# Rows of two weight loads shared out unevenly over the transfer engines, a load in halves and a combination moved ahead, in a fused decoder step

## The reference

```python
def run(args):
    xb, e = args
    z = xb @ w_up[e] + b_up[e]
    x_glu = jnp.minimum(z[:, ::2], SWIGLU_LIMIT)
    x_lin = jnp.clip(z[:, 1::2], -SWIGLU_LIMIT, SWIGLU_LIMIT)
    y = x_glu * jax.nn.sigmoid(SWIGLU_ALPHA * x_glu) * (x_lin + 1.0)
    return y @ w_down[e] + b_down[e]
...
out = jnp.zeros((T + 1, D_MODEL), jnp.float32).at[buf_tok].add(yb * buf_w[:, None])[:T]
```

## Time and profile before

| | |
|---|---|
| time, median of 3 runs | 1134.8 us (1134.33 to 1135.38) |
| the profiled execution's own time | 1134.97 us |
| its span, first to last instruction | 1133.2 us |
| granted PE clock, mean | 0.999 |
| PE busy | 1103.4 us (97%) |
| DVE, ACT, POOL busy | 28%, 20%, 3% |
| moved by DMA | 437.99 MB, mean 387 GB/s |

### The profile page before, as it was taken

The page is one execution under the profiler, slowest core; times in us unless marked ns, Lnnn a source line. Parts: engine busy times, 40 slices in busy tenths (PEclk is TensorE's granted clock), DMA queues, the critical chain, the costliest instruction groups (busy, mean ns, idle before and its releaser), DMA issues.

```text
span 1133.2 us, 14624 instructions
## 1 busy us (share of the span) xinstructions
PE 1103.4 (97%) x5774; PEld 491.7 (43%) x5774; DVE 313.6 (28%) x794; ACT 228.7 (20%) x635; POOL 34.6 (3%) x71
## 2 busy tenths in 40 slices
PE   9999999999999999999999999999999999999997
PEld 6788878844243333333433333333332323233322
DVE  6565662122212121213221313030303021212123
ACT  3663454412020101010101010111110101010103
POOL 1200012200000000000000000000000000000000
PEclk9999999999999999999999999999999999999999
DMA  9743528999999999999999999999999999999995
GB/s 349 292 162 116 166 105 341 408 397 421 429 427 430 436 427 430 433 429 431 422 426 434 427 431 436 428 430 437 428 430 436 429 430 436 429 426 428 427 423 235
DMA packets 31263, 437.99 MB, mean 387 GB/s; under 512 B 5616, under 2 KB 7944, under 8 KB 10360
## 3 DMA queue, kind: packets, MB, share of 16 engines
q1 hardware_dynamic: 30592, 435.64, 91.7%
q10 hardware_dynamic: 624, 1.68, 0.4%
HBM read 436.00 MB, written 2.41 MB: 387 GB/s over the span
## 4 chain that ended last, share of the span: by engine, by line
PE 73%; DMA 22%; DVE 2%; issue 1%; ACT 1%; SPq 0%; DVEq 0%
PE bank L1407 26%; DMA ring<-in_experts 21%; PE bank L1445 16%; PE bank L1113 10%; PE bank L1159 5%; PE bank L1303 4%; PE bank L1282 3%; PE bank L1227 1%; PE bank L1316 1%; PE bank L1306 1%; DVE area L1861 1%; PE bank L1279 1%; PE bank L984 1%; PE bank L995 1%; DMA ring<-in_opening 1%
## 5 line engine op out<-in xcount | busy, mean ns | idle before, releaser
L1407 PE MATMUL bank<-ring,area 128*64 128x512 f32 x1872 | 424.7, 597 | 7.3 <-DMA ring<-in_experts 6.9
L1407 PEld LDWEIGHTS bank<-ring,area 128*64 128x64 f32 x1872 | 126.6, 136 | 276.2 <-issue 254.0
L1445 PE MATMUL bank<-ring,area 128*64 128x512 f32 x960 | 220.6, 599 | 5.9 <-DMA ring<-in_experts 5.8
L1849 DVE TENSOR_TENSOR x_tok<-x_tok,bank 128x512 f32<-128x512 f32 x60 | 41.3, 688 | 326.6 <-PE bank L1303 326.6
L862 ACT ACTIVATE area<-area 128x256 f32<-128x256 f32 x64 | 26.7, 417 | 513.7 <-DVE area L1861 513.7
L1113 PE MATMUL bank<-ring 128*128 128x264 f32 (+1 forms) x512 | 119.6, 391 | 0.0
L1445 PEld LDWEIGHTS bank<-ring,area 128*64 128x64 f32 x960 | 63.5, 136 | 122.8 <-issue 107.2
L1113 PEld LDWEIGHTS bank<-ring 128*128 128x128 f32 x512 | 95.8, 190 | 20.0 <-issue 1.3
L1886 DVE TENSOR_TENSOR area<-area 128x1024 f32<-128x1024 f32 x15 | 18.4, 1225 | 209.5 <-ACT area L872 209.5
L1303 PE MATMUL bank<-area 128*128 128x512 f32 x128 | 71.8, 644 | 0.0
L1159 PE MATMUL bank<-area,ring 128*128 128x264 f32 x256 | 58.6, 387 | 0.0
(11 more groups left out here) (292 smaller groups left out, 685.6 us busy)
## 6 DMA issues: line engine op xcount, KB each, us to landing
ring<-in_experts SPq DMA_DIRECT2D x64, 4096.0 KB, 24.9
ring<-in_experts SPq DMA_DIRECT2D x36, 2048.0 KB, 30.4
ring<-in_experts SPq DMA_DIRECT2D x24, 1024.0 KB, 9.0
ring<-in_w_in SPq DMA_DIRECT2D x16, 1024.0 KB, 9.5
area<-in_experts SPq DMA_DIRECT2D x7, 2048.0 KB, 13.1
area<-in_experts SPq DMA_DIRECT2D x3, 4096.0 KB, 20.8
ring<-in_w_out SPq DMA_DIRECT2D x8, 1024.0 KB, 4.8
area<-in_experts SPq DMA_DIRECT2D x4, 1024.0 KB, 8.3
```

The source lines that it names most:

```text
L1407: m = mm(bank[2 * h + n][64 * e:64 * e + 64, :], xe[:, k, 64 * e:64 * e + 64], w[:, kk, e, NB * n:NB * (n + 1)], start=False, stop=(k == K ...
L1445: m = mm(bank[4 + c][64 * e:64 * e + 64, :], y_t[:, 4 * half + f, 64 * e:64 * e + 64], w[:, f, e, :], start=False, stop=(half == 1 and f = ...
L1849: eng.tensor_tensor(x, x, combined_bank(unit, last)[:, :], ALU.add).then_inc(s.added, 1)
```

## The change

Three edits, all for the last pair.

- Loads 185 and 186 become three transfers each: rows 0 to 111, rows 112 to 119 and rows 120 to 127, all on the load's own semaphore, which is now counted to 48 (`signals` gives 3).
- Load 188 becomes two transfers, its first and its second half of columns; the second counts on a semaphore of the opening (`open_loaded[0]`, used once before) and PE waits for it ahead of `f` = 2. `y_rows(q, 1)` moves from before `f` = 3 to before that wait.
- `combine(q, 2)` moves from behind the last matmul of load 191 to ahead of that load's last quarter (`f` = 3), before the wait for it.

```diff
+SHARED = (185, 186)
+EVEN_ROWS, FEW_ROWS = 112, 8
...
-    return 3 if n == WIDE + 1 else 2 if WIDE <= n <= WIDE + HALVED else 1
+    return 3 if n == WIDE + 1 or n in SHARED else 2 if WIDE <= n <= WIDE + HALVED else 1
...
+            def shared_dma(n, dst, full):
+
+                for lo in (0, *range(EVEN_ROWS, P, FEW_ROWS)):
+                    rows = slice(lo, EVEN_ROWS if lo == 0 else lo + FEW_ROWS)
+                    eng.dma_start(dst[rows, :], source(n)[rows, :]).then_inc(full, 16)
...
-                if i <= UP_LOADS:
+                if n in SHARED:
+                    shared_dma(n, dst, full)
+                elif i < UP_LOADS:
                     expert_dma(n, dst, full)
+                elif i == UP_LOADS:
+
+                    piece(n, dst, full, 0, SLOT // 2)
+                    piece(n, dst, open_loaded[0], SLOT // 2, SLOT)
...
-                        if last and i and f == 2:
+                        if last and i == 0 and f == 2:
+                            y_rows(q, 1)
+                            eng.wait_ge(open_loaded[0], 32)
+                        elif last and f == 2:
                             if i == 2:
                                 combine(q, 0, True)
                             eng.wait_ge(half_full[i - 1], 16)
                         if last and i == 3 and f == 3:
+                            combine(q, 2, True)
                             eng.wait_ge(s.front_full, 32)
-                        if i == 0 and f == 3:
+                        if i == 0 and f == 3 and not last:
                             y_rows(q, 1)
...
-            for unit in LAST_ORDER[1:]:
+            for unit in LAST_ORDER[2:]:
                 combine(PAIRS - 1, unit, True)
```

## The result

The changed kernel takes 1154.8 us (median of 4 runs, 1154.05 to 1155.87), the kernel before 1134.9 (4 runs beside it, 1134.33 to 1135.38). The ratio is 1.0176, interval 1.0163 to 1.0188: slower by 19.9 us. The forecast was slower by 7.3 us, 1142.1, with a range up to 1144.5. The direction was right, the size was not, and the time lies outside the range. The profiled execution took 1155.12 us, with a span of 1153.2 (before 1133.2), so the two traces can be set against each other nearly one to one: 20.0 us.

The account below looks back on a forecast made before the run. Load arrivals up to 188 and PE's work behind them were taken to bound the kernel. Arrivals 6.6 us late plus 0.7 for the moved combination gave +7.3 us on the median 1134.8, 1142.1 us; range 1134.2 to 1144.5.

Parts of the forecast that it names:

- What bounds the kernel: At the end: arrivals of loads up to 188, then PE's own work behind them, later loads just in time.
- the 112-row part at full rate: Loads 185 and 186: rows 0 to 111 give each engine 7 rows at 0.61 us.
- the late eight: Loads 185 and 186: extra rows fall on engines behind, full price, +9.4 us, 1144.2; chance 0.17 shared with a slowed 112-row part.
- the 112-row part slowed too: Loads 185 and 186: the 112-row transfers also lose rate, 1144 us and above; chance 0.17 shared with the late eight.
- The 8-row part: Loads 185 and 186: each 8-row transfer takes 2.50 us, as the rate falls with the number of rows written.
- L: Lateness of all arrivals from load 186 on: 8.7 us less a 2.1 us lead, 6.6 us.
- The lead of 2.1 us: End of the loads: eight engines finish up to 2.1 us ahead, covering part of the cost if given the extra rows.
- Arrivals: Load 185 late by 2.3 us, 186 by 6.6; PE idle about 2.4 and 4.7 us; nothing made up behind.
- PE's clock: Rival: the clock falls in PE's new idle gaps, perhaps a further microsecond; counted in the slow case, no chance of its own.
- Edits 2 and 3: Load 188 in halves: nothing (0 to -0.8 us); unit 2's combination moved ahead: +1.06 and -0.35, net +0.7 us.
- SP's issues at nothing: SP's extra transfer issues, 0.33 to 0.42 us each, cost nothing, hidden by over 31 us before landing.
- The other side: Rival: narrow transfers cost nothing extra and extra rows fall on engines ahead; -0.2 us, 1134.6 us; chance 0.24.

Follow-up runs that it names:

- The 64-row halves: Loads 185 and 186 each as two transfers of 64 rows, otherwise the kernel before: 1150.32 us, 15.3 late.
- the pair on lower and upper rows: Kernel before with load 185 as eight 8-row transfers, four apart, other half left out: rows 0 to 63 1133.57 us, rows 64 to 127 1144.09 us.
- edit 1 alone: Kernel before with only loads 185 and 186 split into 112 + 8 + 8 rows: 1154.21 us, 18.9 late.

## Why the prediction was right in direction and wrong in size

**What bounds the kernel: right.** Two limits, the arrivals and PE's work behind them. After the change the arrivals set the time up to load 186, and PE alone from there.

**The step that failed: the 112-row part at full rate.** The sum took 7 x 0.61 us for it, that is no loss, and gave only the chance of a rival (0.17, with the late eight) to "the 112-row part slowed too". Alone it costs 11.9 us for two loads, and the rest of edit 1 another 7.0. I had read in the earlier trace rows that the rate follows from the rows written, and had applied this to the number of rows only: 112 of 128 looked like nearly all. The 64-row halves and the pair on lower and upper rows show that it matters which rows a transfer moves and not how many; for the 112 rows themselves, that engines meet at the same rows is inferred from these runs. A smaller slip in the reading of the early stage: 8 KB a row holds for its 256 KB loads, the 128 KB loads have 4 KB a row.

**The 8-row part: about the right size, on the wrong ground.** The forecast had L = 6.6 us for all of edit 1, and in it the 8-row transfers stand at 10.0 us (four at 2.50), less the rows that the 112-row part saves and less the lead. As 16 rows in one piece the rest costs 3.5 us, as 8 + 8 it costs 7.0 (18.9 - 11.9). That 6.6 and 7.0 lie close together is luck: the ground (few rows, whatever rows) is refuted by the eight transfers, four rows apart, that cost nothing on rows 0 to 63. The direction was forecast on the same wrong ground.

**The lead of 2.1 us, the gain from sharing out unevenly: not seen.** No run shows this term by itself. The end of the loads, kernel after (columns as above), to be set beside the earlier trace rows:

```profile
1133.00:1134.00 1.00, 1.00 (x8) 0.15 (x4) 0.00 (x0) 0.31 (x1) 0.00 (x0) 1.00 0.88 356
1134.00:1135.00 1.00, 1.00 (x4) 0.30 (x2) 0.00 (x0) 0.00 (x0) 0.00 (x0) 1.00 0.78 315
1135.00:1136.00 1.00, 1.00 (x5) 0.34 (x6) 0.49 (x1) 0.00 (x0) 0.00 (x0) 1.00 0.35 139
1136.00:1137.00 1.00, 1.00 (x6) 0.29 (x4) 0.90 (x2) 0.00 (x0) 0.00 (x0) 1.00 0.12 49
1137.00:1138.00 1.00, 1.00 (x8) 0.35 (x6) 0.00 (x0) 0.00 (x0) 0.00 (x0) 1.00 0.08 33
```

The shares were 0.90, 0.56, 0.43, 0.22; now 0.88, 0.78, 0.35, 0.12, 0.08 and then 0.02. Most engines end closer together than before, but one or two run on for longer, and a load is there only when its last engine is. Whether a balance could be won at all stays open; with transfers of 112 or of 8 neighbouring rows it cost more here than the 2.1 us it could have given.

**Arrivals.** Load 185 late by 2.3 and 186 by 6.6 was forecast; their starts are late by 11.8 and 18.6. Load 184, which I had left untouched, is late by 5.4. Idle time ahead of them: forecast 2.4 and 4.7, measured 5.48 (184), 4.92 and 4.41. "All arrivals behind are late by the same, nothing is made up" was right up to load 187.

**PE's clock: a rival's remark, and a term of the measured sum.** I had put one further microsecond on it. The three loads take 1.6, 2.8 and 1.7 us longer. The first two are covered by the next wait; the third, ahead of load 187 whose data is there, is on the path: 1.7 us.

**Edits 2 and 3: right.** Forecast +0.7, alone +1.1 (0.1 to 2.2). The waits stood where forecast, unit 4 followed at 0.70 us (forecast 0.75). In the changed kernel, too, they cost 0.9 us between load 187 and unit 4 against edit 1 alone (21.92 against 21.01), and edit 2 gives nothing there, because load 188 is no longer awaited with it or without it. One reading was loose: the waits of the earlier trace rows are those of PE's weight loads. PE itself stood still for hardly anything there in the kernel before (24 matmul records in 5.48 us, where 5.37 is the time without a wait); it is the earlier start that runs into the arrivals.

**SP's issues at nothing: right.** Of the four transfers more for loads 185 and 186, two put an issue of 0.33 us each ahead of the last transfer of load 185 on the chain (the lines of L483 above); the 45.85 us to landing behind them are set by the stream. SP's other issues in the kernel after, same view as the earlier trace rows:

```profile
L487 SPq DMA_DIRECT2D ring<-in_experts x9: 327/538/14980, 1071.5 to 1112.8; - x9
...
DMA to landing us min/median/max: 26.1/51.3/53.5
```

One issue took 14.98 us (4.24 was the longest before), while the stream was slow, and a piece still lands 26.1 us or more after its issue. Behind load 186 PE never stood waiting for a load, so these late issues cost nothing.

**The rivals.** The other side (an 8-row transfer under about 1.2 us, 1134.6) did not come about in the change, though its ground, no price for narrowness, is just what the lower rows show for rows four apart. "The 112-row part slowed too", with 1144 and above and a share of the 0.17, is the one that came. Which engines got the extra rows stays open.

## What to carry to other kernels

In a stream like this one, which keeps all transfer engines busy, leave every transfer in the shape that spans all 128 rows; to cut a load, cut its columns (halves and quarters cost nothing measurable here), not its rows. If a change introduces a new shape, price each of its pieces by a row of its own, the large ordinary-looking one first: it carries most of the bytes. And a busy share near 1 doesn't say that transfers run at their rate: read it beside GB/s.

## What the runs showed of the hardware that I had not expected

- Transfers of 112 or 64 rows ran at 187 to 226 GB/s with the engines' share at 1, against 428 for whole loads.
- Eight transfers of 8 rows cost nothing on rows 0 to 63 (-0.6 us, within the spread) and 9.9 us on rows 64 to 127, in the same stream; a row took 0.61 us there and 1.26 here.
- Such a transfer slows loads issued ahead of it: load 184 started 4.4 us late with the upper rows and 5.4 us late in the changed kernel.
- With 64 and 64 rows PE's granted clock was 0.50 (the lower level, 1.2 GHz) from 1110 to 1115 us, behind 4.91 us of idle time, and load 186 took 6.62 us in place of 3.65.
